# Staging the q and k products of a hybrid trunk layer in SBUF, with squares and casts on GpSimd

## The reference

```python
h = modulate(rms_norm(x, lp['g_mix']), sh2, sc2)
proj = h @ lp['w_in']
p = proj[..., :o1]
q = rms_norm(proj[..., o1:o2].reshape(B, L, N_HEADS, HEAD_DIM), lp['q_gain'])
k = rms_norm(proj[..., o2:o3].reshape(B, L, N_HEADS, HEAD_DIM), lp['k_gain'])
v = proj[..., o3:o4].reshape(B, L, N_HEADS, HEAD_DIM)
...
a = pool_mixer(p, lp['w_pool'], lp['pool_scale']) @ lp['w_br_pool']
# att: dense attention (context) or neighbourhood attention plus cached keys (latent)
b = att @ lp['w_br_att']
merged = gates[:, :, 0] * a + gates[:, :, 1] * b
x = x + g2 * (merged @ lp['w_out'])
```

## Time and profile before

| | us |
|---|---|
| median of 3 runs | 1688.66 (1687.80 to 1692.62) |
| profiled execution | 1701.97 |
| its span (core 3, the slowest) | 1700.4 |
| spans of the other cores | 1680.7 to 1699.9 |
| TensorE busy, share of the span | 1536.0, 90% |
| VectorE busy | 956.5, 56% |
| ScalarE busy | 494.2, 29% |
| GpSimd busy | 158.2, 9% |

### The profile page before, as it was taken

The page is one execution under the profiler, slowest core; times in us unless marked ns, Lnnn a source line. Parts: engine busy times, 40 slices in busy tenths (PEclk is TensorE's granted clock), DMA queues, the critical chain, the costliest instruction groups (busy, mean ns, idle before and its releaser), DMA issues.

```text
span 1700.4 us, 25281 instructions; the slowest of 8 cores (1680.7 to 1700.4 us)
## 1 busy us (share of the span) xinstructions
PE 1536.0 (90%) x8548; PEld 695.4 (41%) x8548; DVE 956.5 (56%) x1646; ACT 494.2 (29%) x739; POOL 158.2 (9%) x235
## 2 busy tenths in 40 slices
PE   1689999999999995698889888999999999999998
PEld 1234444444444442243434444444334444444443
DVE  2256556555566554464546665345366666666666
ACT  2651110111111125745636566235421111111110
POOL 2131000000000012300000000021210000000000
PEclk9799999999999997787889899999999999999999
DMA  9906442345432332457225355584322222222005
GB/s 183 243 1 91 75 67 37 48 74 76 75 48 43 59 87 99 101 116 142 37 56 120 99 113 113 138 186 75 50 38 38 37 38 38 38 38 38 13 1 198
DMA packets 35788, 134.68 MB, mean 79 GB/s; under 512 B 5072, under 2 KB 5200, under 8 KB 33616
## 3 DMA queue, kind: packets, MB, share of 16 engines
q0 software_dynamic: 22560, 79.88, 30.3%
q1 hardware_dynamic: 13104, 53.18, 9.3%
HBM read 191.95 MB, written 20.97 MB: 125 GB/s over the span
## 4 chain that ended last, share of the span: by engine, by line
PE 79%; DVE 6%; issue 5%; ACT 4%; DMA 4%; POOL 1%; DVEq 0%; ACTq 0%; SPq 0%; POOLq 0%
PE ps L413 76%; ACT arena L422 3%; DVE arena L430 3%; PE ps L410 3%; DMA arena<-wts 3%; DVE arena L426 2%; POOL arena L603 1%; DMA arena<-xin 1%; DVE arena L436 1%; ACT L422 1%; DVEq L183 0%; DVE arena L445 0%; DVE arena L442 0%; ACTq L183 0%; POOL arena L323 0%
## 5 line engine op out<-in xcount | busy, mean ns | idle before, releaser
L413 PE MATMUL ps<-arena 128*128 128x512 bf16 (+3 forms) x7108 | 1476.7, 363 | 132.9 <-DVE arena L430 53.5
L413 PEld LDWEIGHTS ps<-arena 128*128 128x128 bf16 x7108 | 646.7, 100 | 919.6 <-issue 336.8
L430 DVE SCALAR_TENSOR_TENSOR arena<-ps,arena 128x512 f32<-128x512 f32 (+2 forms) x860 | 562.5, 714 | 89.6 <-ACT arena L422 47.1
L422 ACT ACTIVATE arena<-ps 128x512 f32<-128x512 f32 (+4 forms) x418 | 266.1, 652 | 1045.8 <-PE ps L413 526.7
L426 DVE TENSOR_TENSOR arena<-arena,ps 128x512 bf16<-128x512 f32 (+1 forms) x198 | 130.2, 658 | 411.7 <-PE ps L413 382.4
L426 DVE TENSOR_TENSOR arena<-arena 128x512 f32<-128x512 f32 (+10 forms) x196 | 141.6, 738 | 114.9 <-ACT arena L422 89.3
L323 POOL DMA_DIRECT2D arena<-wts x150 | 79.9, 536 | 1255.5 <-PE ps L413 1025.0
L422 ACT ACTIVATE arena<-arena 128x512 bf16<-128x512 f32 (+6 forms) x230 | 165.6, 748 | 86.9 <-DVE arena L426 25.0
L410 PE MATMUL ps<-arena 128*128 128x65 bf16 (+3 forms) x1440 | 80.6, 214 | 25.5 <-DVE arena L436 16.0
L603 POOL TENSOR_TENSOR arena<-arena 128x512 bf16<-128x512 f32 (+3 forms) x77 | 75.9, 1010 | 186.4 <-ACT arena L422 99.3
L410 PEld LDWEIGHTS ps<-arena 64*128 64x128 bf16 (+1 forms) x1440 | 53.5, 98 | 79.0 <-issue 69.8
(11 more groups left out here) (12 smaller groups left out, 6.1 us busy)
## 6 DMA issues: line engine op xcount, KB each, us to landing
arena<-wts POOLq DMA_DIRECT2D x150, 512.0 KB, 8.8
arena<-xin SPq DMA_DIRECT2D x8, 1024.0 KB, 13.6
xspill<-arena SPq DMA_DIRECT2D x4, 2048.0 KB, 7.0
arena<-xspill SPq DMA_DIRECT2D x4, 2048.0 KB, 14.7
yoT<-arena SPq DMA_DIRECT2D x32, 256.0 KB, 2.3
arena<-ebias SPq DMA_DIRECT2D x12, 640.0 KB, 5.1
arena<-ebias SPq DMA_DIRECT2D x8, 768.0 KB, 5.4
nkT<-arena SPq DMA_DIRECT2D x8, 256.0 KB, 2.9
```

What stands on the lines that cost most here:

```text
L413: return P.emit("pe", lambda e: e.matmul(out, lhsT=lhsT, rhs=rhs, start=start, stop=stop), reads=reads, writes=writes, inc=inc)
L422: return P.emit("act", lambda e: e.activation(out=out, in_=in_, func=func, **kw), reads=reads, writes=writes)
L430: return P.emit("dve", lambda e: e.scalar_tensor_tensor(out=out, in0=in0, scalar=scalar, in1=in1, op0=op0, op1=op1), reads=reads, writes=w ...
```

## The change

Each q or k product is copied out of its bank at once, by VectorE (even products) or ScalarE (odd ones), into one of eight float32 staging buffers STG, which frees the bank. GpSimd squares it from there. The summing matmul, Ln, Exp and scaling come two products later instead of one, and the scaling reads the staging buffer. For the context k it works in place, GpSimd makes the bfloat16 copy, and new_k is written from the same buffer. The v products of the context half use the same eight buffers, with the cast on GpSimd. SQ grows from two buffers to four, RSQ shrinks from three to two; STG takes the place of KNF and VST.

```diff
-        SQ = mem(oG, 2048, BF16, "p (s t) -> p s t", s=2)
-        RSQ = mem(oG + 2048, 6144, F32, "p (s t) -> p s t", s=3)
-        KNF = mem(oG + 8192, 8192, F32, "p (s t) -> p s t", s=4)
-        VST = mem(oG + 16384, 8192, F32, "p (s t) -> p s t", s=4)
+        SQ = mem(oG, 4096, BF16, "p (s t) -> p s t", s=4)
+        RSQ = mem(oG + 4096, 4096, F32, "p (s t) -> p s t", s=2)
+        STG = mem(oG + 8192, 16384, F32, "p (s t) -> p s t", s=8)
...
+        def stg_next():
+            s = qcnt["s"] % 8
+            qcnt["s"] += 1
+            return STG[:, s, :], P.R("stg", s), "stg%d" % s
+
+        def pcopy(out, in_, reads, writes):
+            return P.emit("pool", lambda e: e.tensor_copy(out=out, in_=in_), reads=reads, writes=writes)
...
-                s = q % 3
+                s = q % 2
...
                 if want_nk:
-                    ks = qcnt["k"] % 4
-                    qcnt["k"] += 1
-                    rk = P.R("knf", ks)
-                    vstt(KNF[:, ks, 0:n], bank_ap(b)[:, 0:n], gain, RSQ[:, s, 0:n], ALU.mult, ALU.mult,
-                         [banks[b], rr, r_mc, r_gains], [rk])
-                    vcopy(out, KNF[:, ks, 0:n], [rk], wres(hp, tl0, n))
-                    out_toks.append(sp_dma(nk_d[:, hp, t0:t0 + n], KNF[:, ks, 0:n], "nk%d" % ks, reads=[rk]))
+                    vstt(st[:, 0:n], st[:, 0:n], gain, RSQ[:, s, 0:n], ALU.mult, ALU.mult,
+                         [rr, r_mc, r_gains], [rst])
+                    pcopy(out, st[:, 0:n], [rst], wres(hp, tl0, n))
+                    out_toks.append(sp_dma(nk_d[:, hp, t0:t0 + n], st[:, 0:n], sem, reads=[rst]))
                 else:
-                    vstt(out, bank_ap(b)[:, 0:n], gain, RSQ[:, s, 0:n], ALU.mult, ALU.mult,
-                         [banks[b], rr, r_mc, r_gains], wres(hp, tl0, n))
+                    vstt(out, st[:, 0:n], gain, RSQ[:, s, 0:n], ALU.mult, ALU.mult,
+                         [rst, rr, r_mc, r_gains], wres(hp, tl0, n))
...
-                        actv(SQ[:, q % 2, 0:n], bank_ap(b)[:, 0:n], AF.Square, [banks[b]], [P.R("sq", q % 2)])
-                        pend.append((b, q, 2 * u + bb, t0, n))
-                        if len(pend) > 1:
+                        stg = stg_next()
+                        st, rst = stg[0][:, 0:n], stg[1]
+                        if q % 2 == 0:
+                            vcopy(st, bank_ap(b)[:, 0:n], [banks[b]], [rst])
+                        else:
+                            actv(st, bank_ap(b)[:, 0:n], AF.Copy, [banks[b]], [rst])
+                        ptt(SQ[:, q % 4, 0:n], st, st, ALU.mult, [rst], [P.R("sq", q % 4)])
+                        pend.append((q, stg, 2 * u + bb, t0, n))
+                        if len(pend) > 2:
                             finish(pend.pop(0))
...
-                    sv = i % 4
-                    rs = P.R("vst", sv)
-                    actv(VST[:, sv, :], bank_ap(b), AF.Copy, [banks[b]], [rs])
-                    vcopy(dst, VST[:, sv, :].rearrange("p (h t d) -> p h t d", h=4, t=2), [rs], [rv])
-                    out_toks.append(sp_dma(nv_d[tk:tk + 128, :], VST[:, sv, :], "vst%d" % sv, reads=[rs]))
+                    st, rs, sem = stg_next()
+                    actv(st, bank_ap(b), AF.Copy, [banks[b]], [rs])
+                    pcopy(dst, st.rearrange("p (h t d) -> p h t d", h=4, t=2), [rs], [rv])
+                    out_toks.append(sp_dma(nv_d[tk:tk + 128, :], st, sem, reads=[rs]))
```

More of the change, by code:

```diff
@@ L830, in rqt @@
             return [P.R("qt", half, hp, i) for i in range(tl0 // 128, (tl0 + n + 127) // 128)]
-        qcnt = {"q": 0, "k": 0}
+        qcnt = {"q": 0, "s": 0}
+        def stg_next():
[4 more added lines that the diff above has]
+            return P.emit("pool", lambda e: e.tensor_copy(out=out, in_=in_), reads=reads, writes=writes)
         def qk_gen(half, nm, dpool, spool, hooks=()):
@@ L847, in finish @@
             def finish(item):
-                b, q, hp, t0, n = item
+                q, (st, rst, sem), hp, t0, n = item
                 b2 = spool.next()
-                mm(bank_ap(b2)[:, 0:n], ONESBLK, SQ[:, q % 2, 0:n], True, True, [P.R("sq", q % 2), r_mc], [banks[b2]],
+                mm(bank_ap(b2)[:, 0:n], ONESBLK, SQ[:, q % 4, 0:n], True, True, [P.R("sq", q % 4), r_mc], [banks[b2]],
                    inc=True)
-                s = q % 3
+                s = q % 2
                 rr = P.R("rsq", s)
@@ L1233, in mixer @@
             P.claim(oX[2] + 8192, 8192, [("kt", 0, hp) for hp in range(4)])
[L1234 to L1237, removed]
+            P.claim(oG, 4096, [("sq", s) for s in range(4)])
+            P.claim(oG + 4096, 4096, [("rsq", s) for s in range(2)])
+            P.claim(oG + 8192, 16384, [("stg", s) for s in range(8)])
             d1, s1 = PsumPool(P, [0, 1, 2, 3, 4, 5], "d1"), PsumPool(P, [6, 7], "s1")
```

## The result

| | kernel before | changed kernel |
|---|---|---|
| median of 3 runs | 1688.66 (1687.80 to 1692.62) | 1707.08 (1705.92 to 1707.42) |
| ratio, 95% interval | | 1.0101 (1.0076 to 1.0127) |
| repeated beside each other, four times | 1 | 1.0036 (1.0022 to 1.0050), 1.0029 (1.0017 to 1.0042), 1.0032 (1.0010 to 1.0054), 1.0033 (1.0021 to 1.0044) |

The change makes the kernel slower. The first measurement lies 13 us above the forecast of 1693.9 and above the range. The repetitions put the changed kernel at 1.0033 of the kernel before, which is 1694.2 on 1688.66.

A forecast was written before the change was run, and what follows sets the result against it. The q stage was taken to go at ScalarE's pace, with gains possible only in TensorE's 29 us of idle time. 5.8 - 0.6 - 1.0 + 1.0 = +5.2 on 1688.66 gave 1693.9 us, range 1682 to 1703.

The forecast's parts named there:

- The base: Whole kernel: sum made on core 0, whose 1687.4 us lies next to the median of the runs, 1688.66.
- Term A: Context half's q stage: first squares wait in GpSimd's queue, last sum 4.0 us later, clock 1.8; +5.8 us (-3.5 to +8).
- rival three: k and v stages: VectorE starves as its two-input work and GpSimd exclude each other; +6 us on forecast, 1700, chance 0.17.
- the stop at 770: TensorE's 4.94 us wait for VectorE before the last pool mix, v stage; forecast to shrink 3 to 5 us.
- Term B: Context half's k stage with pool projection: copies free banks that late scalings held; -0.6 us (0 to -1.4).
- The burst: Left-over sums at a product stage's end, one matmul each with stops between; in the latent half forecast at +1.5 us.
- Term C: v stage with pool projection: casts leaving VectorE give 2.6 us, less collisions with GpSimd; net -1.0 us (-6.7 to +3).
- Term D: Latent half's q, k, v beside context attention: flush +1.5, freed bank -1.2, VectorE copies +0.7; +1.0 us (-3 to +4).
- signs set down for failure: Wrong if q-stage holes sum to under 2 us, or GpSimd casts take under 0.5 us and the 770 stop goes.
- the holes of the q stage: TensorE's stops in the context half's q stage, 3.50 and 3.23 us before; under 2 us in sum would refute the forecast.
- No wait for the scaling line in the k stage: Context half's k stage: expected sign that TensorE's waits for banks held by late VectorE scalings, 1.4 us, disappear.

The follow-up runs named there:

- e_carry: Changed kernel with the context half's q stage as before and sums left at a stage's end worked off behind the next stage's first products: 1681.66 us, ratio 0.9963.
- e_castgp: Kernel before with only its sixteen casts of k and v moved from VectorE to GpSimd: ratio 1.0003.
- e_lag: Kernel before with only statistics and scaling two products behind instead of one, without staging copies: 1744.41 us, ratio 1.0323.

## Why the prediction was wrong

**The base.** The step that failed is in the first paragraph: core 3 "ran the stages of interest at a lower granted clock, which the change doesn't touch", so the sum was made on core 0 and laid on 1688.66. The change doesn't touch it, but a median can hold it or not. The earlier trace rows showed that an execution with the stretch ends 14 us later, and the profiled execution beside three timed runs showed it in one of four. That was a case with its own price, forecast + 13, 1707, and at one in four per execution a chance of some 0.16 for the median of three; it was neither a rival nor in the range.

**Term A, forecast +5.8, measured +7.0.** The mechanism held event by event. With 1.57 added, GpSimd's first square starts at 701.77 behind the three weight issues (forecast 701.8), the sum of product 0 at 703.09 (702.9), the halo squares end at 706.05 (706.2; the last 1.03 of the seven squares' 5.31 is product 2's). The three last stops sum to 6.3 us (6.4). What was too small lies between: from the halo's Ln to the copy of product 5, 710.55 to 718.53, it took 8.0 us, where 7.3 was carried over from before, and the last sum came 5.65 later than its 720.78 (4.0). VectorE's scalings in this stage met GpSimd's squares; the one at 714.19 lies on that way:

```profile
703.78 2.28 DVE L430 SCALAR_TENSOR_TENSOR arena<-arena 128x512 bf16<-128x512 f32 x1 [5.67 <-ACT arena L422]
...
714.19 1.58 DVE L430 SCALAR_TENSOR_TENSOR arena<-arena 128x512 bf16<-128x512 f32 x1 [0.27 <-ACT arena L422]
...
720.50 0.75 DVE L430 SCALAR_TENSOR_TENSOR arena<-arena 128x512 bf16<-128x512 f32 x1 [2.16 <-ACT arena L422]
```
```profile
714.19 2.17 POOL L603 TENSOR_TENSOR arena<-arena 128x512 bf16<-128x512 f32 x2 [3.66 <-DVE arena L442]
```

The prediction took this operation's price as that of the old one to some hundredths. Alone it is (0.75), beside GpSimd it was 1.58 and 2.28. By the rule of the Trainium skill, SBUF — State Buffer, section Who interferes with whom, it had joined the operations that exclude GpSimd's reads; these rows agree. As rival three it was priced too high: the stop at 770 shrank.

**Term B, forecast -0.6, measured +2.2.** The wrong sign. The waits for banks did go, as forecast. But the term's last sentence gave the square "7 us of matmuls to hide in", and that holds for the products in the middle only. The burst that A and D priced was left out for k: stops of 0.88 and 2.17 where 0.47 and 0.68 were. e_carry removes them, and k falls to 26.1.

**Term C, forecast -1.0, measured -1.8.** Right in mechanism for the stop: 4.94 became 3.47. The 18 matmuls behind it, which the term left at 6.29, took 4.04, at a granted clock of 1.00 from 778 to 783 where before had 0.65 from 770 to 777. A GpSimd cast takes, from the page's form list of core 0, more than I took (0.7):

```profile
L839 POOL CAST arena<-arena 128x512 bf16<-128x512 f32 x16 | 16.0, 1002 | 17.4 <-ACT arena L422 13.0 <-DVE arena L430 4.5
```

Undisturbed it is 0.61 (743.49), between the bounds, and 1.60 at most, beyond them. That the casts as such are worth nothing (e_castgp) the prediction didn't see either; their worth of 4.6 us in the changed kernel is that they pay for the copies.

**Term D, forecast +1.0, measured -2.3.** The burst cost what it was said to and more (ScalarE waits 4.6 instead of 1.5, forecast +1.5), but all waits for banks in this half went, 1.4 and 1.5, not the 1.23 alone, and the waits for attention's VectorE work (L442 and L436) fell from 9.1 to 7.8, where +0.7 was forecast. Waits of TensorE from 776 to 868, core 0, changed kernel:

```profile
PE ps L413 <- ACT arena L422: 4.6, 5, 1.1
PE ps L410 <- DVE arena L436: 4.2, 2, 2.2
PE ps L410 <- DVE arena L442: 3.6, 3, 2.3
PE ps L413 <- DVE arena L430: 3.5, 1, 3.5
```

(The last is the stop at 778, which belongs to v.) e_lag shows how near this half is to its three banks.

The four terms sum to +5.2 and measured +5.1, with merge and the rest +5.3. That is luck in part: errors of +1.2, +2.8, -0.8 and -3.3 cancel. Neither of the signs set down for failure came: the holes of the q stage grew, and the stop at 770 stayed. "No wait for the scaling line in the k stage" was met too, but the time went to a line that it didn't list.

## What to carry to other kernels

A longer lag between a product and its statistics does not remove the chain behind the last products. It leaves more of it for the end of the stage, where nothing covers it; carry what is left into the next stage's products, and keep the lag short where the stage is bound by the engine that makes the copies. A copy that frees a bank early paid where banks are few (three, the latent half) and cost where there were six (the q stage). When one execution among the few shown has a core pair at a lower clock, give that case a chance and a price of its own.

## What the runs showed of the hardware

A third level of the clock. Over 58 us core 4 had 0.79 granted with TensorE busy 51 of them, core 6 had 0.94, and eight matmuls took 2.28 against 1.90 us, a ratio of 0.83; neither 1.2 nor 2.4 GHz fits that row. In a window without a long stop the level stands alone, core 5 and then core 6:

```profile
780.00:793.00 13.00, 12.76 (x60) 0.81 0.78 157
```
```profile
780.00:793.00 13.00, 12.18 (x70) 1.00 0.82 156
```

The Trainium skill, TensorE: Matmul & The Clock Gate, Part 1, section Seeing it yourself, tells of a limiter at 13/16 (0.81) that takes a whole die once three of its cores run dense matmuls. The level agrees. The extent in this execution doesn't: all eight cores ran the same program, a pair of one die had it for some 160 us, the other pair of that die did not, and in the 84 undisturbed executions of the two kernels since, on three chips, it was in none.

A cast of 128x512 from fp32 to bf16 on GpSimd takes 0.61 us alone and 1.00 on average in this kernel, a square 1.04. One and the same kernel has a v stage of 22.3 us on one core and 24.3 on another (e_castgp, cores 0 and 1): the stop before the last pool mix was 3.03 and 3.65 us, and the 18 matmuls behind it took 5.44 and 6.81, with the granted clock of 752 to 776 at 0.93 and 0.86. A gain of 2 us in one core's stage is not yet a gain.
